# One TensorE loop over experts 6 to 29 in a MoE layer: the residual added by VectorE, the down bias in steps 4 and 5

## What is computed

```python
x = x + concat(retention, moba) @ w_out
h = rms_norm(x, norm2_w)
top_logit, top_e = top_k(h @ w_router + b_router, 4)     # of 32 experts
gate = softmax(top_logit)
# for each expert e, over the tokens that chose it:
u = h[tok] @ w1[e] + b1[e]                               # 1024 -> 2048
y = clamped_swiglu(u) @ w2[e] + b2[e]                    # 1024 -> 1024
acc[tok] += y * gate
x = x + acc
out = rms_norm(x, final_norm_w)
```

## Time and profile before

| | us |
| --- | --- |
| median of 3 runs | 1031.92 |
| lowest, highest | 1031.69, 1032.65 |
| the profiled execution | 1031.34 |
| its span | 1029.6 |
| TensorE busy | 1017.1 |
| VectorE busy | 263.0 |
| ScalarE busy | 129.6 |

### The profile page before, as it was taken

One profiled execution on the slowest core, in us unless ns is written; L12 is line 12 of the kernel. 1 busy time (PEld: TensorE's weight loads), 2 busy tenths in 40 slices (PEclk: granted clock), 3 DMA queues, 4 the chain that ended last, 5 costly groups with the idle time before them and its releaser, 6 DMA issues.

```text
span 1029.6 us, 11656 instructions
## 1 busy us (share of the span) xinstructions
PE 1017.1 (99%) x4910; PEld 409.6 (40%) x4910; DVE 263.0 (26%) x636; ACT 129.6 (13%) x256; POOL 0.2 (0%) x4
## 2 busy tenths in 40 slices
PE   9999999999999999999999999999999999999996
PEld 8888433333333333333333333333333333333332
DVE  6878642111111111111111111111111111111111
ACT  2433220000000000000000000000000000000002
POOL 0000000000000000000000000000000000000000
PEclk9999999999999999999999999999999999999999
DMA  9985999999999999999999999999999999999996
GB/s 327 366 342 200 422 361 424 427 427 425 436 433 428 428 432 434 433 430 430 432 433 431 430 432 430 432 434 432 432 430 432 434 432 432 429 433 427 426 424 260
DMA packets 36382, 424.25 MB, mean 412 GB/s; under 512 B 3224, under 2 KB 16160, under 8 KB 19840
## 3 DMA queue, kind: packets, MB, share of 16 engines
q1 hardware_dynamic: 36048, 423.51, 97.7%
q10 hardware_dynamic: 304, 0.33, 0.1%
HBM read 422.78 MB, written 1.05 MB: 412 GB/s over the span
## 4 chain that ended last, share of the span: by engine, by line
PE 90%; DMA 8%; DVE 0%; issue 0%; ACT 0%; DVEq 0%; ACTq 0%
PE PS L2036 40%; PE PS L2059 19%; DMA ring<-in_w 8%; PE PS L1612 7%; PE PS L2002 5%; PE PS L1984 5%; PE PS L1872 3%; PE PS L1826 2%; PE PS L2094 2%; PE PS L1994 2%; PE PS L1976 1%; PE PS L1579 1%; PE PS L2169 1%; PE PS L1556 0%; PE PS L2189 0%; PE PS L1719 0%
## 5 line engine op out<-in xcount | busy, mean ns | idle before, releaser
L2036 PE MATMUL PS<-ring,work 128*64 128x512 f32 x1976 | 431.8, 594 | 1.9 <-DMA ring<-in_w 1.9
L2036 PEld LDWEIGHTS PS<-ring,work 128*64 128x64 f32 x1976 | 140.2, 137 | 271.3 <-issue 266.6
L2059 PE MATMUL PS<-ring,work 128*64 128x512 f32 x1024 | 227.5, 595 | 0.8 <-DMA ring<-in_w 0.7
L2059 PEld LDWEIGHTS PS<-ring,work 128*64 128x64 f32 x1024 | 71.5, 137 | 153.8 <-issue 149.7
L1455 DVE TENSOR_SCALAR work<-PS 128x512 f32<-128x512 f32 x32 | 22.1, 692 | 387.1 <-PE PS L2036 387.1
L925 ACT ACTIVATE work<-work 128x512 f32<-128x512 f32 x32 | 20.2, 631 | 517.5 <-DVE work L1455 517.5
L1418 DVE TENSOR_TENSOR work<-PS,n2w 128x512 f32<-128x512 f32 x30 | 20.8, 692 | 229.8 <-PE PS L1994 229.8
L1612 PE MATMUL PS<-ring 128*128 128x256 f32 (+1 forms) x336 | 70.7, 364 | 0.0
L2002 PE MATMUL PS<-late,work 64*128 64x512 f32 x248 | 61.9, 616 | 0.0
L1612 PEld LDWEIGHTS PS<-ring 128*128 128x128 f32 x336 | 57.9, 190 | 7.7 <-issue 1.3
L1984 PE MATMUL PS<-resid,work 128*64 128x512 f32 x248 | 58.6, 593 | 0.0
(11 more groups left out here) (210 smaller groups left out, 463.7 us busy)
## 6 DMA issues: line engine op xcount, KB each, us to landing
ring<-in_w SPq DMA_DIRECT2D x72, 4096.0 KB, 30.2
ring<-in_w SPq DMA_DIRECT2D x34, 2048.0 KB, 12.9
ring<-in_w SPq DMA_DIRECT2D x22, 1024.0 KB, 8.7
ring<-in_w_in SPq DMA_DIRECT2D x11, 1024.0 KB, 12.1
ring<-in_w SPq DMA_DIRECT2D x10, 512.0 KB, 5.1
ring<-in_w_out SPq DMA_DIRECT2D x4, 1024.0 KB, 11.2
work<-in_w SPq DMA_DIRECT2D x1, 1024.0 KB, 7.1
out<-resid SPq DMA_DIRECT2D x3, 256.0 KB, 3.4
```

Source lines behind the costliest of these rows:

```text
L2036: last = mm(bank(b0 + v)[64 * half:64 * half + 64, :], rows[:, c, :], turned_half(w[:, v * F:(v + 1) * F], half), start=(second and c == 0 ...
L2059: last = mm(out[64 * half:64 * half + 64, :], aT_n[:, c, 64 * h:64 * h + 64], ring[:, 2 * d + c // 2, cols:cols + BANK], start=(h == 0 and ...
```

## The change

1. TensorE runs the 12 turns as one loop. `add_and_read` goes; the register load of the count is done in step 30 by `read_most`, as on the other engines.
2. The residual is added by VectorE in step 3 (`add_resid`): four additions in place in banks 2, 3, 6, 7, after the sums of step 2 (`combined`). TensorE waits for them (`resid_added`) before it sums in step 3.
3. The down bias is added by TensorE in step 4 for tile 0 and in step 5 for tile 1, after `combine`.
4. VectorE's loop gets `head_slot=0`: its first instruction is put at the border of a block of its instruction memory, and the code ahead jumps there.
5. Three semaphores of the first memsets become one, `set_ready`, with thresholds 1, 2 and 3.

The core of the diff:

```diff
-PE_LOOPS, DVE_LOOPS = [(0, 4), (4, ITERS)], [(0, ITERS)]
+RESID_STEP, BIAS_STEPS = 3, (4, 5)
...
-        def run_experts(eng, step, r, loops=(), between=None):
+        def run_experts(eng, step, r, rolled=False):
...
-            if loops:
-                for n, (first, end) in enumerate(loops):
-                    if n:
-                        between()
-                    with eng.Fori(first, end) as i:
-                        for j in range(PEEL, PEEL + UNROLL):
-                            step(r, i, j)
-            elif isinstance(r, int):
+            if isinstance(r, int) and not rolled:
...
-                with eng.Fori(0, ITERS) as i:
+                slot = {eng.engine: 0} if rolled and eng.engine == mybir.EngineType.DVE else None
+                with nc.Fori(0, ITERS, engines=[eng.engine], head_slot=slot) as i:
...
+            def add_resid():
+
+                dve.wait_ge(combined, 2 * T * (RESID_STEP - 1))
+                for t in range(T):
+                    for half in range(2):
+                        b = bank(2 + 4 * t + half)
+                        nc.vector.tensor_tensor(b, b, resid[:, t, half_cols(half)], ALU.add).then_inc(resid_added, 1)
...
                 if not late_put:
                     make_pickg(e)
+                if isinstance(r, int) and j == RESID_STEP:
+                    add_resid()
...
-            run_experts(dve, expert_dve, 0, DVE_LOOPS)
+            run_experts(dve, expert_dve, 0, rolled=True)
...
+                if isinstance(r, int) and j == RESID_STEP:
+                    pe.wait_ge(resid_added, 2 * T)
                 if j > 0:
                     combine(putb, y_sb, (0, 1))
+                if isinstance(r, int) and j in BIAS_STEPS:
+                    add_down_bias(BIAS_STEPS.index(j))
+                read_most(pe, "pe", r, i, j)
                 pe.wait_ge(gh_ready, n + 2)
                 put_transposes(n + 1, bank(4))
...
-            def add_and_read():
-
-                add_down_bias()
-                add_resid()
-                read["pe"] = pe.value_load(most_i[0:1, 0:1], min_val=0, max_val=SEQ)
...
-            def add_down_bias():
+            def add_down_bias(t):
 
                 pe.wait_ge(gatesT_ready, 1)
...
-            run_experts(pe, expert_pe, 0, PE_LOOPS, add_and_read)
+            run_experts(pe, expert_pe, 0, rolled=True)
```

## The result

| | before | after |
| --- | --- | --- |
| median, us | 1031.74 | 1033.18 |
| runs | 22 | 22 |
| lowest, highest, us | 1030.06, 1032.65 | 1031.92, 1034.92 |
| span of the profiled execution, us | 1029.6 | 1030.2 |

The ratio is 1.0015, with a 95% interval of 1.0009 to 1.0021. The changed kernel is **slower by about 1.4 us**, 0.14%. That lies inside the 0.2% called "the same" and inside the range 1029.8 to 1033.4, but the forecast was a gain of 0.9 us, and the interval excludes it. The profiled execution of the changed kernel is one of its quicker ones: its span is 0.6 us longer than before, so its trace shows less than half of the difference. All times here are of executions with a granted clock above 0.99; one of e5's six took 1500.04 us at 0.653 and is left out.

A forecast was written before the change was run, and what follows sets the result against it. The prediction took the weight transfers, landing on their own clock through a full queue, as the bound, not TensorE. Terms 0 + 0 - 0.9 = -0.9 us took the median from 1031.9 to 1031.0 us, range 1029.8 to 1033.4.

The forecast's parts named there:

- What the lateness costs: Loads issued at 272.2 and 299.6, TensorE 1.8 and 3.6 us later: landings don't move, cost 0.
- above 13.3, so the landings don't move: Criterion at those two loads: times to landing of 13.6 and 13.7 us stay above the shortest, 13.3.
- from 244.8 on the queue is never empty: SyncE's load queue: landings run on their own clock, 9.71 us each, and TensorE's speed doesn't set it.
- the fetches: Second TensorE loop's code, loads 28 to 33: one loop removes two fetches; between 0 and 0.9 us, 0.9 taken.
- the alignment, put at 0: VectorE's loop on a block border: one jump at step 6, beside idle time, cost 0.
- no gain from the fetches: Rival: other code blocks still fetched may delay the same DMA engine; time stays 1031.9 us; chance 0.28.
- the ring runs dry: Rival: clock falls in steps 4 and 5, loads near 272.2 and 299.6 shift by 3.0 us; 1034.0; chance 0.07.
- TensorE doesn't set the end: From step 14 on TensorE is 5.33 us earlier but waits for landings that don't come earlier; gain 0.
- Its waits for weights grew as forecast: After step 14, TensorE's total waits grow from 2.6 to about 7 us, from about three steps before step 29.
- The residual on VectorE costs nothing that shows: Step 3: four additions, 2.8 us, fit in VectorE's 12.42 us of idle time before its clamp; cost 0.
- The register load: Step 30: TensorE's read of the count, 487 ns, stands behind running sums or later waits; cost 0.
- the end moves with the 72nd landing: The end is last landings plus a fixed tail of matmuls, sums and stores; 72nd load landing near 948.3.

The follow-up runs named there:

- e5: Changed kernel with the down bias matmuls of steps 4 and 5 done twice each; 1036.53 us, ratio 1.0055.
- e10: Changed kernel with eight written-out steps instead of six and the bias in steps 6 and 7; 1033.41 us, ratio 1.0019.
- e13: Changed kernel with eight written-out steps instead of six and the down bias left out; 1033.09 us, ratio 1.0015.
- e12: Changed kernel with the bias as two concurrent pairs of matmuls in different row groups, both in step 5; 1031.56 us, ratio 1.0001.
- e14: The kernel of e12 measured a second time; 1031.47 us, ratio 1.0001.
- e2: Changed kernel with the bias as pairs of matmuls in different row groups, half 0 in step 4, half 1 in step 5; 1032.13 us, ratio 1.0005.
- e9: The changed kernel itself measured again as a control; 1032.48 us, ratio 1.0009.
- e4: Kernel before with only the bias moved to steps 4 and 5; two loops and the residual between them stay; 1032.35 us, ratio 1.0009.
- e8: Changed kernel without putting VectorE's loop on a block border; 1032.81 us, ratio 1.0013.
- e3: Kernel before with only the residual moved to VectorE in step 3; two loops and the bias between them stay; 1031.70 us, ratio 1.0003.
- e7: Kernel before with TensorE's 12 turns in six loops of two turns instead of two loops; 1032.67 us, ratio 1.0012.
- e11: Changed kernel with the whole down bias in step 30; 1033.56 us, ratio 1.0018.
- e1: Changed kernel with the down bias left out; 1031.34 us, ratio 1.0001.
- e6: Kernel before with neither residual nor down bias, its two TensorE loops kept; 1031.55 us, ratio 1.0000.

## Why the prediction was wrong, and where it was right

**The step that failed** is "What the lateness costs". The issue times were nearly right: 1.9 and 3.8 us of lateness where 1.8 and 3.6 stood, plus the 0.5 of the head. The times to landing came out above those forecast, 14.0 and 14.9 against 13.6 and 13.7. The criterion was wrong: "above 13.3, so the landings don't move". They moved by 0.5 us between the 1st and 4th load and by 0.8 more up to the 7th (by the rows' tenths). Two faults lie in it. First, 13.3 us was the time of a load issued at 244.8, when some DMA engines had already run low: before, 8 of their packets took more than 1.35 us there and they stood idle for 2.0 us together. It is alike in every kernel whose first 4 MB load stands there (all but e10 and e13). So 13.3 marks a point beyond the limit, not the limit, and "from 244.8 on the queue is never empty" didn't hold for each engine. Second, a load of 4 MB is 128 packets over 16 DMA engines, each with its own requests, and it counts as landed when the slowest is done. Time to landing is that of the fullest engine; the emptiest one can idle long before it shows.

A better measure can be read from the same rows: what is left when the load is issued, the landing of the load before it minus the issue. Before, for the 7th load, the 6th was issued at 288.8:

```profile
L582 SPq DMA_DIRECT2D ring<-in_w x1: 328/328/328, 288.8 to 288.8; - x1
...
DMA to landing us min/median/max: 18.1/18.1/18.1
```

Left were 288.8 + 18.1 - 299.6 = 7.3 us. In the changed kernel the 6th load is issued at 291.2:

```profile
L575 SPq DMA_DIRECT2D ring<-in_w x1: 328/328/328, 291.2 to 291.2; - x1
...
DMA to landing us min/median/max: 16.6/16.6/16.6
```

Left were 291.2 + 16.6 - 303.8 = 4.0 us. Over the kernels the picture is the same, worked out in this way. How much later the load lands than at the full rate is its landing minus the one before, less 9.71. The packet records tell the same of each engine, since each marks its share of a load as done with a packet of 4 bytes: what the emptiest engine had left at the issue, and how much time was lost per engine (idle and in slow packets, as above).

| kernel, 4th and 7th load | left at issue, us | emptiest engine, us | lands later, us | lost per engine, us |
| --- | --- | --- | --- | --- |
| before | 5.4, 7.3 | 3.3, 5.1 | 0.2, 0.2 | 0.0, 0.0 |
| e12 | 5.6, 5.4 | 3.3, 3.1 | 0.0, 0.3 | 0.0, 0.0 |
| e14 | 5.5, 5.4 | 3.3, 3.1 | 0.0, 0.0 | 0.0, 0.0 |
| e2 | 5.7, 6.5 | 2.2, 3.5 | 0.1, 0.2 | 0.9, 0.0 |
| changed | 3.8, 4.0 | 1.4, 1.6 | 0.5, 1.2 | 0.4, 0.8 |
| e9 | 4.3, 4.2 | 1.4, 1.8 | 0.1, 1.2 | 0.5, 0.7 |
| e4 | 3.7, 4.3 | 1.5, 1.7 | 0.9, 0.6 | 0.6, 0.7 |
| e8 | 3.8, 3.6 | 1.3, 1.4 | 0.0, 3.1 | 0.3, 0.8 |
| e5 | 0.2, 1.7 | -2.1, -0.3 | 2.2, 2.3 | 3.3, 2.0 |

Where the emptiest engine has 3.1 us or more, nothing is lost to packets that follow a low queue; at 2.2 us and below something always is. How late the load then lands is a matter of chance around 4 us. e2's 4th load shows why the landing alone isn't enough: 5.7 us were left on the slowest engine, 2.2 on the emptiest, and 0.9 us per engine were lost without the landing showing it. With more left, loads still slip, by 0.5 to 1.6 us (e3, e7, e10, e11, e13), each time within 11 us behind an instruction packet; such packets also stand close to the 4th and 7th load in every kernel of the table, so part of the 0.5 and 1.2 us can be theirs. The trace of the kernel before gave 5.4 and 7.3, and with the lateness forecast 5.4 - 1.8 = 3.6 and 7.3 - 3.6 = 3.7 for the change. What it didn't give is the limit; the prediction had only "with little to spare".

**The term that was mis-sized** is the fetches. The 0.9 us vanished from loads 28 to 33 as forecast, and no instruction packet stands between 500 and 900, where SyncE's queue is the only one:

```profile
q1 hardware_dynamic: 5942, 172.82, 100.4%
```

But the prediction left the value open between 0 and 0.9 us and took 0.9, from one execution. Over many executions one loop instead of two brings 0.2 to 0.5 us inside the span, and a fetch costs 0.13 us (e7). And **the alignment, put at 0**, costs 0.4 us outside the span (e8), which the prediction didn't look at. Together they leave nothing of the gain: e1 has 1031.34 us where the kernel before has 1031.50. The rival "no gain from the fetches" was the nearer one.

The errors add up: forecast -0.9, measured +1.4, 2.3 us apart. From e1 the changed kernel differs by the bias alone, and 1033.18 - 1031.34 = 1.8 us is what the bias costs (1.1 with the median of e9), where 0 was forecast. The alignment is 0.4 and the fetches 0.4 to 0.7 of the rest; the sum of the three, 1.9 to 2.9, takes in the 2.3.

**The rival "the ring runs dry"** had the mechanism and, with 1034.0, a price 0.8 us too high. Its cause was wrong for this change: it needed the clock to fall in steps 4 and 5 and lateness past 4.0 us. The clock stayed at 1.00 there (every stretch read from 265 to 276 and 294 to 304), and 3.8 us were enough. Nor did the ring run dry: the loss was for the most part in slow packets. With eight records in a row its cause does arise (e5). The Trainium skill (page "TensorE: Matmul & The Clock Gate", section "Part 1: The HAM clock gate") names idle time as what throttles the clock; the eight bias records of the earlier trace rows, of e5 after step 4 and of e11 speak against it: TensorE was busy in the whole of those stretches and the clock fell. But eight of them are not enough by themselves either: in the traces of e3 and of e5 after step 5 it didn't fall, and in e11 only some executions have the lower mean clock.

**What held.** TensorE doesn't set the end: 5.3 us less of it (e3) and 9.0 us less, in one loop (e1) or in two (e6), all leave the time where it was. Its waits for weights grew as forecast to about 7 us. Two of them in its timeline, and the sums of the waits (us, times, longest):

```profile
853.01 7.09 PE L2039 MATMUL PS<-ring,work 128*64 128x512 f32 x32 [1.51 <-DMA ring<-in_w]
...
940.43 4.94 PE L2039 MATMUL PS<-ring,work 128*64 128x512 f32 x22 [1.50 <-DMA ring<-in_w]
...
PE PS L2039 <- DMA ring<-in_w: 6.2, 5, 1.5
...
PE PS L2062 <- DMA ring<-in_w: 0.6, 1, 0.6
```

6.2 + 0.6 = 6.8 us, against 2.6 in the earlier trace rows. They begin at 853.01, in step 26: three steps before step 29, as forecast.

The residual on VectorE costs nothing that shows. Its timeline in step 3, the four additions and the clamp:

```profile
211.75 2.49 DVE L1432 TENSOR_TENSOR PS<-PS,resid 128x512 f32<-128x512 f32 x4
...
224.79 0.69 DVE L1458 TENSOR_SCALAR work<-PS 128x512 f32<-128x512 f32 x1 [10.03 <-PE PS L2039]
```

2.49 us of additions (2.8 forecast), and still 10.03 us of idle time before the clamp, against 12.42 in the earlier trace rows. Step 14 begins here:

```profile
515.64 9.66 PE L2039 MATMUL PS<-ring,work 128*64 128x512 f32 x44
```

515.6 where 515.0 was forecast, the rest is the head. The register load took 482 ns behind running sums and brought no wait. That the end moves with the 72nd landing held in most kernels, where the last weights land 68.8 to 69.2 us behind it, but not in e12 and e14 (70.1 and 70.4).

The 72nd load landed at 950.1, where 948.3 was forecast: 949.2 + 0.5 by the head + 1.3 of new loss - 0.9 by the fetches.

**Open.** Which DMA engine runs low, and so whether 0 or 3 us are lost at 4 us of reserve, differs between executions; nothing here controls it. Differences below about 1 us between two experiments lie within their intervals. What eight written-out steps do to the tail isn't settled, nor why a packet behind a low queue takes up to 2.85 us, nor what the 0.4 us outside the span are.

## What to carry to other kernels

In a kernel whose transfers are the bound, a microsecond taken from a compute engine is worth nothing, and a microsecond added to it early, while the ring has little queued, can cost a whole one: move added work to where the queue is deep and the end is far, or make it short. Read the reserve as the landing of the load before minus the issue of this one, better still by the emptiest engine, and compare it with a load that surely found all engines supplied, not with the shortest time to landing in the trace. Look at the time outside the span too: a trace that shows a gain can belong to a kernel that has none. A small loss seen at one place in one execution is not yet a gain to be had; multiply its suspected cause (as e7 does) before counting on it.

## What the runs showed of the hardware

- A load over 16 DMA engines with deep queues is not one stream. The engines' last packets of a load end up to 3 us apart (945.8 to 948.7 in the packet records of the kernel before, 1.7 us for the 3rd load), so a disturbance of one engine can cost between nothing and its full length.
- A DMA engine whose queue runs low loses time before it is idle: with 1.3 to 2.2 us left on the emptiest engine at the issue of the next load, 8 to 25 packets of 32 KB took over 1.35 us instead of 1.21, up to 2.85; with 3.1 us or more, two at most (4th and 7th loads).
- A fetch of 16 KB of code holds one DMA engine for about 1.1 us and cost 0.13 us on average in e7 (0.03 to 0.24 by the interval).
- Putting VectorE's loop on a block border added 0.4 us outside the profiled span (2.20 against 1.82 us) with six written-out steps, and none with eight.
- Eight bias records (32 rows, 128 columns, one behind the other) were followed by a fall of the granted clock to 0.50 (before), 0.57 (e5, after step 4) and 0.54 (e11), with TensorE busy throughout. Eight were not in e3 and in e5 after step 5, nor the eight that run side by side in 1.99 us in e12, nor four (steps 4 and 5 of the changed kernel). It also differs between executions of one kernel: e11's have mean clocks of 0.995 to 0.998. What decides is open.
